# Stage A of a hybrid attention kernel: another order on ScalarE and VectorE, and late modulation products two rounds earlier

## The reference, cut to what matters

```python
mod = jax.nn.silu(c) @ w_ada + b_ada                 # six vectors of 1024 for each sequence
h = _rmsnorm(x, norm1_g) * (1.0 + sc1) + sh1         # uses the first two
proj = h @ w_in                                      # 8192 columns, q|k|v of A, q|k|v of B, two gates
...
qa = _partial_rope(_rmsnorm(qa, a_qnorm_g), pos)     # A: 8 heads, two 64-wide maps for each
ka = _partial_rope(_rmsnorm(ka, a_knorm_g), pos)
p = jax.nn.softmax(jnp.where(mask, s, NEG_INF), axis=-1)
a = p[:, :, 0] - lam * p[:, :, 1]
outs.append(jnp.einsum('bhqk,bkhd->bqhd', a, vf[:, :kend]))
...
return _rmsnorm(o, subln_g) * (1.0 - lam_init)
```

## Time and profile before

| | |
|---|---|
| median of 3 runs | 859.41 us (856.08 to 861.2) |
| the profiled execution | 860.19 us, span 858.5 us |
| mean granted TensorE clock over the span | 0.933 of full speed |
| stage A, from the first projection product to the mix | about 39.8 to 242.3 us of the span |
| busy: PE, DVE, ACT, POOL | 714.1, 347.3, 270.1, 102.1 us |

### The profile page before, as it was taken

The page is one execution under the profiler, slowest core; times in us unless marked ns, Lnnn a source line. Parts: engine busy times, 40 slices in busy tenths (PEclk is TensorE's granted clock), DMA queues, the critical chain, the costliest instruction groups (busy, mean ns, idle before and its releaser), DMA issues.

```text
span 858.5 us, 13770 instructions
## 1 busy us (share of the span) xinstructions
PE 714.1 (83%) x5329; PEld 586.5 (68%) x5329; DVE 347.3 (40%) x539; ACT 270.1 (31%) x490; POOL 102.1 (12%) x161
## 2 busy tenths in 40 slices
PE   0798888899799799999988999736998888788770
PEld 0487777788599798999987999634654554545440
DVE  0656555556534334333442356541233113213225
ACT  1454455454335254444544442300111011101100
POOL 2011111111000001010010000010011100100014
PEclk9899999999899899999999999857999999999985
DMA  9966466555643666452315443499899999999805
GB/s 323 321 167 197 132 181 176 174 172 175 195 152 111 175 172 226 118 139 63 110 44 163 147 133 113 165 424 416 324 418 417 418 418 418 417 417 419 332 17 183
DMA packets 131176, 199.17 MB, mean 232 GB/s; under 512 B 11688, under 2 KB 113464, under 8 KB 117816
## 3 DMA queue, kind: packets, MB, share of 16 engines
q1 hardware_dynamic: 123032, 185.63, 61.1%
q0 software_dynamic: 6208, 11.02, 3.6%
q10 hardware_dynamic: 1888, 1.86, 0.7%
HBM read 193.47 MB, written 16.55 MB: 245 GB/s over the span
## 4 chain that ended last, share of the span: by engine, by line
PE 52%; issue 22%; ACT 9%; DVE 8%; DVEq 3%; POOL 2%; POOLq 2%; ACTq 1%; DMA 0%
PE ps L551 29%; PE ps L546 6%; PE ps L548 6%; PE ps L547 6%; ACT w_hi L1069 3%; DVE w_lo L1365 2%; ACT probs L1151 1%; PE ps L948 1%; PE ps L952 1%; PE ps L984 1%; ACT probs L1127 1%; DVE amap L1425 1%; DVEq L1450 1%; PE ps L716 1%; DVE ss L1433 1%
## 5 line engine op out<-in xcount | busy, mean ns | idle before, releaser
L551 PE MATMUL ps<-e_w,xgT 128*64 128x256 f32 x1024 | 130.2, 418 | 31.9 <-issue 30.7
L551 PEld LDWEIGHTS ps<-e_w,xgT 128*64 128x64 f32 x1024 | 91.8, 151 | 66.1 <-issue 37.4
L1365 DVE TENSOR_TENSOR w_lo<-raw,w_hi 128x2048 fp32r<-128x2048 f32 (+1 forms) x36 | 100.5, 2793 | 86.2 <-ACT w_hi L1069 86.2
L546 PE MATMUL ps<-hT_hi,w_hi 128*128 128x320 f32 x320 | 102.7, 321 | 5.5 <-DVE w_lo L1365 5.2
L548 PE MATMUL ps<-hT_hi,w_lo 128*128 128x320 f32 x320 | 100.0, 312 | 0.0
L547 PE MATMUL ps<-hT_lo,w_hi 128*128 128x320 f32 x320 | 99.9, 312 | 0.0
L1069 ACT ACTIVATE w_hi<-raw 128x2048 fp32r<-128x2048 f32 (+1 forms) x36 | 83.2, 2310 | 28.5 <-PE ps L548 28.5
L1686 DVE TENSOR_SCALAR h_s<-h_e 128x256 f32<-128x256 f32 x16 | 4.7, 294 | 162.3 <-ACT h_e L1282 162.3
L546 PEld LDWEIGHTS ps<-hT_hi,w_hi 128*128 128x128 f32 x320 | 61.2, 191 | 7.9 <-DVE w_lo L1365 5.5
L547 PEld LDWEIGHTS ps<-hT_lo,w_hi 128*128 128x128 f32 x320 | 61.2, 191 | 0.0
L548 PEld LDWEIGHTS ps<-hT_hi,w_lo 128*128 128x128 f32 x320 | 61.1, 191 | 0.0
(11 more groups left out here) (258 smaller groups left out, 1225.6 us busy)
## 6 DMA issues: line engine op xcount, KB each, us to landing
e_w<-in_w SPq DMA_DIRECT2D x96, 1024.0 KB, 18.3
raw<-in_w_in SPq DMA_DIRECT2D x45, 512.0 KB
ada_late<-in_w_ada SPq DMA_DIRECT2D x16, 1024.0 KB, 5.0
ada_first<-in_w_ada SPq DMA_DIRECT2D x8, 1024.0 KB, 21.3
raw<-in_w_in SPq DMA_DIRECT2D x8, 1024.0 KB
raw<-in_w_oa SPq DMA_DIRECT2D x4, 1024.0 KB
raw<-in_w_ob SPq DMA_DIRECT2D x4, 1024.0 KB
raw<-in_w_out SPq DMA_DIRECT2D x4, 1024.0 KB
```

Of the source, the lines that this page charges most:

```text
L546: nc.tensor.matmul(out, lhs_hi, rhs_hi, start=first, stop=False, skip_group_check=True)
L551: return nc.tensor.matmul(out, lhs, rhs, start=first, stop=last, skip_group_check=True)
L1365: V.tensor_tensor(w_lo[j][:, :, 0:width], raw[j][:, :, 0:width], f32(w_hi[j][:, :, 0:width]), ALU.subtract).then_inc(split_done, 1)
```

## The change

1. ACT's order within a round: the split copy moves from behind `rs` to behind `oT_hi`, and is done in two halves around the copy `qkT`. The copy of the sample tile and `osq` now stand ahead of the root of `ss`. `osq` gets a place of its own (it shared that of `sq`).
2. DVE's order within a round: the sums `o_ss` stand ahead of the scaling of `stage`; `w_lo` is made in two halves.
3. The late modulation products run in rounds 1 to 8 in place of 3 to 10. Product 0 stands behind the products with the values in both; product 1 stands ahead of the transposes into bank 3 in place of between those into bank 3 and bank 4. On SP each late load is issued one loop step earlier, so load_late(h) in step h.
4. `late_rows` lies in columns of `xnT` and `h_sample` in its padding, with the same work.

```diff
@@ SP
             a_weights(0, 0)
+            for n in range(2):
+                load_late(0, n)
             a_weights(1, 1)
             a_store(0, 0)
             for n in range(2):
-                load_late(0, n)
+                load_late(1, n)
             with sp.Fori(1, 3) as i:
                 for j in range(2):
                     a_weights(2 * i + j, j)
                     a_store(2 * i + j - 1, 1 - j)
                     a_cache_load(2 * i + j, j, False)
                     for n in range(2):
-                        load_late(2 * i + j - 1, n)
+                        load_late(2 * i + j, n)
...
@@ PE
-                pe.wait_ge(late_in[n], 16 * (h - 2))
+                pe.wait_ge(late_in[n], 16 * h)
...
                     last.then_inc(a_pv, 1)
-                    pe.wait_ge(a_staged, min(3 * h, 24) if isinstance(h, int) else 3 * h)
-                    if not (isinstance(h, int) and h == 3):
-                        pe.wait_ge(late_out, l)
+                if qk_on:
+                    pe.wait_ge(a_staged, 3 * h)
+                    if not (isinstance(h, int) and h == 1):
+                        pe.wait_ge(late_out, h - 1)
                     ada_chunk(h, 0)
...
                 if qk_on:
+                    ada_chunk(h, 1)
                     m = h - 1
                     pe.wait_ge(a_roped, m + 1)
...
                     if o_on:
-                        ada_chunk(h, 1)
                         pe.wait_ge(a_olo, h - 2)
...
-                elif o_on:
-                    ada_chunk(h, 1)
@@ ACT
-                if loaded is not None:
-                    split(jq, loaded, None if isinstance(h, int) and h == 0 else (a_proj, 3 * h),
-                          MIX_COLS if isinstance(h, int) and h >= 7 else UNIT)
...
+                width = MIX_COLS if isinstance(h, int) and h >= 7 else UNIT
+                if loaded is not None:
+                    split_first(jq, loaded, None if isinstance(h, int) and h == 0 else (a_proj, 3 * h), width)
                 if qk_on:
                     act.wait_ge(a_qkT, h)
                     A(qkT[:, 0:512], ps[:, 3, :], ACT.Copy).then_inc(a_qkT_act, 1)
+                if loaded is not None:
+                    split_second(jq, width)
@@ DVE
+                if o_on:
+                    dve.wait_ge(a_osq, h - 2)
+                    V.tensor_reduce(o_ss[:], osq[:], AX, ALU.add).then_inc(a_oss, 1)
+                if qk_on:
                     dve.wait_ge(a_rs, h)
...
                 if split_on:
-                    split(h + 1, jq, MIX_COLS if isinstance(h, int) and h >= 7 else UNIT)
+                    width = MIX_COLS if isinstance(h, int) and h >= 7 else UNIT
+                    for n, (signal, value) in enumerate(((split_half, h + 1), (split_hi, h + 2))):
+                        ks = slice(n * KD // 2, (n + 1) * KD // 2)
+                        dve.wait_ge(signal, value)
+                        last = V.tensor_tensor(w_lo[jq][:, ks, 0:width], raw[jq][:, ks, 0:width], f32(w_hi[jq][:, ks, 0:width]),
+                                               ALU.subtract)
+                    last.then_inc(split_done, 1)
```

More of the change, by code:

```diff
@@ L151, in build @@
         sq = take("sq", [P, TILES, 256])
-        osq = place("osq", [P, TILES, P], F32, cursor[0] - 4 * TILES * 256)
         ss = take("ss", [P, 12])
@@ L165, in build @@
         a_rec = take("a_rec", [P, 2, 3])
+        osq = take("osq", [P, TILES, P])
         o_ss = take("o_ss", [P, 3])
@@ L169, in build @@
         o_n = take("o_n", [P, TILES, P])
-        h_sample = take("h_sample", [P, KD, DEC])
         a_end = cursor[0]
@@ L177, in build @@
         assert ada_at[4] + 8 * D + 2 * D <= raw_at
-        late_rows = place("late_rows", [P, D], F32, hT_at - 4 * KD * PADDED)
+        late_rows, h_sample = xnT[:, :, 0:P], xnT[:, :, TOK:PADDED]
         ada_late = [take(f"ada_late{n}", [P, KD, ADA_COLS]) for n in range(2)]
@@ L286, in build @@
         h_mod = sem("h_mod"); h_hi = sem("h_hi"); h_ready = sem("h_ready")
-        split_hi = sem("split_hi"); split_done = sem("split_done");
+        split_half = sem("split_half"); split_hi = sem("split_hi"); split_done = sem("split_done");
         a_cache = [sem(f"a_cache{j}") for j in range(2)]
@@ L432, in _ @@
                 for n in range(2):
-                    load_late(5 + j, n)
+                    load_late(6 + j, n)
             a_store(7, 1)
-            for n in range(2):
-                load_late(7, n)
             def mix_loads(gate_col, prj, s0, c):
@@ L738, in _ @@
             for n in range(8):
-                last = nc.tensor.transpose(ps[:, 5 + n // 4, (n % 4) * P:(n % 4 + 1) * P], late_rows[:, n * P:(n + 1) * P], ident)
+                last = nc.tensor.transpose(ps[:, 5 + n // 4, (n % 4) * P:(n % 4 + 1) * P], late_rows[:, n, :], ident)
             last.then_inc(col_T, 1)
@@ L1069, in split, with split_first, split_second @@
                 A(w_hi[j][:, :, 0:width], raw[j][:, :, 0:width], ACT.Copy).then_inc(split_hi, 1)
+            def split_first(j, loaded, used, width):
+                act.wait_ge(raw_loaded[j], loaded - 48 * (1 - j))
+                if used is not None:
+                    act.wait_ge(*used)
+                A(w_hi[j][:, 0:KD // 2, 0:width], raw[j][:, 0:KD // 2, 0:width], ACT.Copy).then_inc(split_half, 1)
+            def split_second(j, width):
+                A(w_hi[j][:, KD // 2:KD, 0:width], raw[j][:, KD // 2:KD, 0:width], ACT.Copy).then_inc(split_hi, 1)
             split(0, None, None)
@@ L1080, in _ @@
                     A(hT_hi[:, ks, t * P:(t + 1) * P], h_full[:, ks, t * P:(t + 1) * P], ACT.Copy).then_inc(h_hi, 1)
-            A(hT_hi[:, :, SEQ:TOK], h_sample[:], ACT.Copy).then_inc(h_hi, 1)
+            A(hT_hi[:, :, SEQ:TOK], h_sample, ACT.Copy).then_inc(h_hi, 1)
             act.wait_ge(lam_dve, 1)
@@ L1115, in stage_out @@
                         A(stage[j][:, t, :], ps[:, t, 0:UNIT], ACT.Copy).then_inc(a_staged, 1)
+                if qk_on:
+                    act.wait_ge(a_staged, 3 * h)
+                    if isinstance(h, int) and h == 1:
+                        act.wait_ge(setup_done, 2)
+                    else:
+                        act.wait_ge(a_ss, h - 1)
+                    A(sq[:], stage[jq][:, :, 0:256], ACT.Square).then_inc(a_sq, 1)
                 if P_on:
@@ L1120, in a_iteration @@
                     act.wait_ge(a_pv, h - 2)
+                    if not (isinstance(h, int) and h == 3):
+                        act.wait_ge(a_oss, h - 3)
                     A(osq[:], ps[:, 7, 0:PADDED].rearrange("p (t c) -> p t c", t=TILES), ACT.Square).then_inc(a_osq, 1)
+                if qk_on:
+                    act.wait_ge(a_ss, h)
+                    if not (isinstance(h, int) and h == 1):
+                        act.wait_ge(a_scaled, h - 1)
+                    root(rs[:], ss_ln[:], ss[:], 64, a_rs)
+                if o_on:
                     act.wait_ge(a_oss, h - 2)
@@ L1138, in a_iteration @@
                     A(qkT[:, 0:512], ps[:, 3, :], ACT.Copy).then_inc(a_qkT_act, 1)
+                if loaded is not None:
+                    split_second(jq, width)
                 if P_on:
                     stage_out(1, 2)
-                if o_on:
-                    act.wait_ge(late_used, 2 * h - 4)
-                    A(late_rows[:, bass.ds((h - 3) * P, P)], ps[:, ADA_BANK, 384:512], ACT.Copy).then_inc(late_out, 1)
+                if qk_on:
+                    act.wait_ge(late_used, 2 * h)
+                    A(late_rows[:, bass.ds(h - 1, 1), :].rearrange("p a n -> p (a n)"), ps[:, ADA_BANK, 384:512], ACT.Copy).then_inc(late_out, 1)
                 if s1_on:
@@ L1400, in _ @@
             dve.wait_ge(h_hi, 5)
-            V.tensor_tensor(hT_lo[:, :, SEQ:TOK], h_sample[:], f32(hT_hi[:, :, SEQ:TOK]), ALU.subtract).then_inc(h_ready, 1)
+            V.tensor_tensor(hT_lo[:, :, SEQ:TOK], h_sample, f32(hT_hi[:, :, SEQ:TOK]), ALU.subtract).then_inc(h_ready, 1)
             dve.wait_ge(rows_in, 144)
@@ L1439, in a_iteration @@
                 if o_on:
-                    dve.wait_ge(a_osq, h - 2)
-                    V.tensor_reduce(o_ss[:], osq[:], AX, ALU.add).then_inc(a_oss, 1)
                     dve.wait_ge(a_ors, h - 2)
```

## The result

The changed kernel takes 900.9 us (median of 4 runs, 898.56 to 903.53); the kernel before took 859.49 us beside it (4 runs). The ratio is 1.0488, interval 1.0454 to 1.0522: slower. The profiled execution took 902.0 us with a span of 900.3.

A forecast was written before the change was run, and what follows sets the result against it. TensorE (PE), busy 83% of the span, was taken to bound the kernel. Rounds 3 to 7 +30.0, round 8 +7.9, rounds 0 to 2 +3.6 and round 10 -0.5 gave about +41 us: 900 us, range 884 to 915.

The forecast's parts named there:

- The wait of the load: Rounds 3 to 8: PE waits 6.3 us each for the late load, issued behind SP's wait for the product with the values.
- the estimate of 4.4 us: Landing time of a 1 MB late load by the skill page's fit; the wait would be 5.7 us in place of 6.3.
- The clock: Rounds 3 to 8: PE's clock falls to half behind each load wait, costing 2.1 us each time.
- Rival 1: The clock doesn't fall behind the load waits: +28 us, 888 us; chance 0.16, including a fall in only some rounds.
- The short waits: PE's waits for o_n and oT_lo vanish: 2.4 us gained in each of rounds 3 to 7, 0.53 in round 8.
- rival 4: Both short waits stay because something other than the split sets osq; hidden unless loads are not late, then about 861 us; 0.02.
- part 1: The new order on ACT and DVE, split copy moved behind oT_hi: gains 2.4 us in each of rounds 3 to 7.
- Round 8: The load wait 6.3 and clock 2.1, less 0.5 for the oT_lo wait: +7.9 us.
- Rounds 0 to 2: Two added products in round 1 cost 3.7 us, less 0.1 in round 0; round 2's are covered by waits: +3.6 us.
- Rounds 9 and 10: Without their late products the mix starts earlier, partly offset by the clock coming back later: -0.5 us.
- Rival 3: Loads are not late, SP passing the cache loads before the product with the values; only the reordering counts: 850 us; chance 0.05.
- both go: Work from osq to oT_lo starts up to 2.78 us earlier, exceeding PE's o_n and oT_lo waits together (2.39), so both vanish.

The follow-up runs named there:

- e1: The changed kernel with the two late loads issued ahead of the two cache loads on SP; 849.55 us, ratio 0.987 to the kernel before.
- e5: The changed kernel with the late loads behind SP's wait for the product with the values but ahead of the cache loads; 893.6 us, ratio 1.0389.
- e4b: The changed kernel with 28 unread identity products on PE ahead of the wait for the load, rounds 3 to 8; 890.35 us, ratio 1.0367.
- e2: The changed kernel with the order of ACT and DVE of the kernel before; 900.27 us, ratio 1.0458.
- e8: The changed kernel with the old order on ACT and DVE and the late loads ahead of the cache loads; 861.76 us, ratio 1.0032.
- e3: The changed kernel's order on ACT and DVE alone, late products (rounds 3 to 10) and loads as in the kernel before; 857.77 us, ratio 0.9974.
- e7: The new order with products in rounds 3 to 10 and loads as before, but product 1 ahead of PE's rope wait; 847.11 us, ratio 0.9846.
- e6: The changed kernel with late products in rounds 2 to 9 and late loads ahead of the cache loads; 848.28 us, ratio 0.9862.
- e9: As e6, with the root of ss ahead of ACT's sample copy in round 1 alone; 843.43 us, ratio 0.981.

## Why the prediction was right, point by point

The time (900 against 900.9), the mechanism and its place were right. That the sum came within 1 us is luck: terms that were off by several us cancelled. The terms:

- **The wait of the load.** Shown by after's rows and by e1: 6.3 us predicted, 7.50, 7.40, 7.10, 7.47, 6.17 and 6.51 measured, 7.0 in the mean. Mis-sized by 0.7, or 4.3 us over six. The issue came 1.4 us behind the product where I had 1.26, and the load landed after 5.1 to 6.0 us, 5.65 in the mean, where the median of the earlier trace rows gave 5.0. e5, with no cache load ahead, shows 4.9 to 5.1, so the cache loads just ahead cost 0.7 us of landing in the mean. In the earlier trace rows they stood ahead too, but the late load followed a_vc by 1.35 us, where it follows by 0.72 in round 6 of after; that this gap is what kept the median at 5.0 no run tests. My lower bound of 5.9 us was a slip: 1.26 and 4.8 make 6.1. The Trainium skill (DMA: Bandwidth & Descriptors, "Anatomy of one DMA") gives the fit behind the estimate of 4.4 us for transfers that GpSimd issues, and these are issued by SP. No ada_late load of any trace landed in less than 4.8 us, so the measurement decides. Its rule to issue early and wait late ("Rules for kernel authors") the runs bear out, 51 us by e1.
- **The clock.** 2.1 us a wait predicted; e4b puts it at 2.06 in rounds 3 to 7, and the work at half clock at 2.2. Single rounds vary from 1.3 to 2.9, so 2.1 holds for the mean alone. It fell in each of the six waits. The Trainium skill (TensorE: Matmul & The Clock Gate, "HAM oscillation — how this bites in real kernels") describes this of a kernel that waits for a load before each tile; the trace agrees, with 0.50 granted at the end of all six waits. Rival 1 is out.
- **The short waits.** 2.4 us a round predicted, 2.72 gone. The number was nearly right, but the reason, the new order, does not hold in this kernel: e2 loses the same waits with the old order. I had written this down under rival 4 and not drawn the conclusion, that part 1 brings nothing as long as the load is late.
- **Round 8.** +7.9 predicted, +7.0 measured: the wait was 6.5, and the clock cost less there: e1's round 8 is 18.06, so 25.84 - 18.06 - 6.51 = 1.27.
- **Rounds 0 to 2.** +3.6 predicted, +3.70 measured.
- **Rounds 9 and 10.** -0.5 predicted, -2.0 measured. Dropping the products from these rounds is enough for it: e8 has that with the old order, and from its mask write of round 8 to its first mix product it is 20.7 us, as in after. But the new order alone is enough too: e3 keeps the products in rounds 9 and 10 and takes 20.1. The two gains don't add.

In sum, rounds 3 to 7 came 2.6 us above their term (the waits 4.2 above, the short waits 1.6 the other way), round 8 0.9 and the tail 1.5 below. Rival 3's time, 850 us, is that of e1, but only partly by its sum: e1's mix starts 12.3 us earlier than that of before, where the rival had 9.4, and the rest of that execution took 4.7 us longer. Two more slips are in the rivals: the loss at which rival 3 decides is 9.4 / 6 = 1.57 us a round, not 1.65, and rival 4 with it is 859.4 - 9.4 + 12.5, about 862 us, not 861 (e8 measured 861.8).

What the prediction did not see: part 1 treated the order as good by itself. e3 against e7 shows that it is worth 10.7 us less with product 1 behind the rope's wait. This changed no number here, since the change moves product 1 as well, but the step "both go" rested on it. And in a kernel without the late load I would have missed the root behind the sample copy in round 1, which e6 and e9 show.

Left open: why the part behind the first mix product takes 616 to 621 us from trace to trace, which is where 3.3 us of e5's gain and 4.7 of e1's are gone in their profiled executions; and why the first load of after landed faster in rounds 7 and 8 (5.1 and 5.4 us) than in rounds 3 to 6.

## What to carry to other kernels

For every load that a change moves nearer to its use, look at what stands ahead of it in the queue of the engine that issues it. If that is a wait for the product right ahead of the load's consumer, the whole landing time becomes idle time, each round, and the clock's loss comes on top. When waits overlap, price an edit with and without the others: the same reordering was worth 0 us behind the late load, some 2 us, not clear of the noise, with product 1 behind the rope (e3), and 12 us with both out of the way.

## What the runs showed of the hardware

- The clock stayed full through an idle of 3.16 us and fell behind ones of 2.63 and 2.99 us. In e7 it fell around one of 1.94 us (0.50 over 63 to 66 us), while e6 kept it through one of 1.97 (1.00 over 62 to 70). So among these idles of 1.9 to 3.2 us the length of the one idle did not decide it. It fell in each of six of 6.2 to 7.5 us (after). Filling such a wait with products that nobody reads kept it, and gained 10.5 us of 900.
- A late load of 1 MB landed in 4.9 to 5.1 us with no cache load just ahead (e5) and in 5.1 to 6.0 with two just ahead (after; round 6: 6.0, the second of the pair 8.1).
- A product of the identity with itself, 128x128 f32, takes two records and 0.227 us; four transposes of the same shape, one record each, take 0.65.
